# A two-layer attention backbone: which engine makes the high parts of the second output weights

## The chip, the cores and the metric

One core of a Trainium2 chip runs the whole program. The metric is the device time of one execution in microseconds (us). TensorE (PE) multiplies, VectorE (DVE), ScalarE (ACT) and GpSimd (POOL) work on tiles of 128 partitions in SBUF, SyncE (SP) issues transfers. Each engine runs its own instructions strictly in the order in which they are written; engines wait for each other through semaphores that count up.

## The reference, cut to what matters

```python
for l in range(DEPTH):                                  # two layers
    h = x * (1.0 + sc) + sh                             # 1024 latent tokens, hc: 256 context tokens
    q, k, v, z = jnp.split(h @ w_in[l], 4, axis=-1)
    ...
    # layer 1: 8 heads, two softmax maps each, 1280 keys
    s = jnp.einsum('bhmqd,bhmkd->bhmqk', q, k).astype(jnp.float32) * scale
    p = jax.nn.softmax(s, axis=-1)
    a = (p[:, :, 0] - lam * p[:, :, 1]).astype(v.dtype)
    y = jnp.einsum('bhqk,bhkv->bhqv', a, v)             # then an RMS norm per head
    ...
    out = (y * jax.nn.silu(z)) @ w_out[l]               # 1024 x 1024 weights
    x_new = _layer_norm(DEEPNORM_ALPHA * x + (1.0 + g) * out, ln_g[l], ln_b[l])
```

The products with `w_in` and `w_out` are made from split operands: each fp32 matrix is written as a high part of reduced precision (`_hi`) and the rest (`_lo = raw - hi`), and three products (hi·hi, hi·lo, lo·hi) are summed in PSUM.

## The kernel before, in words

The second layer (`differential`) runs in eight chunks, one head each. A chunk projects its q, k, v and gate and then walks over eight query tiles of 128 rows. The last chunk (`last`) has no next chunk to project for, so it prepares the output projection instead: eight row blocks `k` of `w_out` are loaded by SP into two staging slots (`OutWeights.load`, `w_raw`), split into `h_hi[:, k]` and `h_lo[:, k]`, and TensorE begins to multiply with them before the attention is over.

A slot is loaded again only when the block that lay in it has been split: block `k` waits for `ready >= k - 1`, that is for the subtraction of block `k - 2`.

The four engines share the loop over query tiles. I call the stretch of TensorE that begins with the first transposes of query tile `t` "tile t", and the time at which it begins T(t). In it TensorE does, in this order: `turn(3t)` (four transposes of the probabilities of tile t into PSUM bank 6), `scores(0, t+2)`, the rest of the values of tile t-1, `turn(3t+1)` (four), `scores(1, t+2)`, values, `turn(3t+2)` (two), values. In the last two tiles `ahead` takes the place of the scores; in tile 6 it is `after.part(pe, 0, 0, 0, 7)`, 21 products with the weight blocks 0 to 6, each block waited for by `out_w.ready`.

ScalarE copies each group of transposes out of the one bank (`evac`, L1828), since the next group may come only then, and makes the exponentials of both maps (`exp`, L1821). `evac(n)` belongs to `turn(n)`. Its order in tile t is `evac(3t)`, `exp(1, t+1)`, `evac(3t+1)`, `exp(0, t+2)`, `evac(3t+2)`; in the source the loop index is one lower for the first two of them.

VectorE finds row maxima (`row_max`, L1917, from PSUM) and subtracts the maps (`combine`, L1929, which reads two operands from SBUF). Its order in tile t is `row_max(0, t+2)`, `combine(t+1)`, `row_max(1, t+2)`. `turn(3t)` waits for `combine(t)`.

GpSimd, beside that, splits the first four token tiles of the already stored heads (`load_y`, `split_head`) and the eight weight blocks:

```python
for k in range(KT):
    out_w.copy_hi(pool, p, k)      # h_hi = cast(w_raw)
    out_w.split_lo(pool, k)        # h_lo = w_raw - h_hi
    if k == 0:
        after.split_head(pool, 1)
    if k >= KT - 2:
        pool.wait_ge(out_w.ready, k + 1)
        after.load_y(pool, k - (KT - 2) + 2)
```

After the loop come the RMS norm of the second half (`variance(1)`, `normalise(1)`), four transposes (`spread`, L2115) and the output projection (`Project.pe_part`).

Of the kernel before, what the change touches and what calls it, by code (L numbers as in the profile page):

```python
# [20 lines left out]
D = 1024  # L21
# [4 lines left out]
NCH = D // P  # L26
# [34 lines left out]
ACT = mybir.ActivationFunctionType  # L61
# [10 lines left out]
CREDIT = 1  # L72
# [955 lines left out]
class OutWeights:  # L1028
# [10 lines left out]
    def load(self, sp, p, k):  # L1039
# [3 lines left out]
            sp.wait_ge(self.ready, k - 1)  # L1043
        sp.dma_start(self.stage[k % 2], self.w_out[self.l, k * P:(k + 1) * P, :]).then_inc(self.loaded[k % 2], 16)

    def copy_hi(self, pool, p, k):
        if k == 0:
            pool.wait_ge(p.proj, CREDIT + NCH * p.G)
        pool.wait_ge(self.loaded[k % 2], 16 * (k // 2 + 1))
        self.nc.gpsimd.tensor_copy(self.m.h_hi[:, k, 0:D], self.stage[k % 2]).then_inc(self.hi, 1)  # L1050
# [633 lines left out]
def differential(nc, m, far, stack, p, tokens, before, all_counters, out_w, after, rope_in, y_out):  # L1684
# [14 lines left out]
    y_ready, y_stored = sem("y_ready"), sem("y_stored")  # L1699

    NQ = LAT_TILES
    KEYS = TOK_TILES
    turns = [(t, a, min(4, KEYS - a)) for t in range(NQ) for a in range(0, KEYS, 4)]
    TPT = 3
# [5 lines left out]
    sum_of = lambda mp, t: m.stats[:, 32 + t:33 + t] if mp == 0 else stat(t, 3)  # L1710
    first_sums = m.stats[:, 32:32 + NQ]
    COEFS = 2 * NQ + 2
    variances, roots, inv_rms = (m.stats[:, 40 + i * NQ:40 + (i + 1) * NQ] for i in range(3))

    def run():
        with nc.Block() as block:
# [38 lines left out]
            @block.gpsimd  # L1755
            def _(pool):
                before.pool_part(pool)
                p.split_lo_part(pool, nc.gpsimd, 0, 0)
                for g in range(3):
                    for k in range(KT):  # L1760
                        if g == 0:
                            pool.wait_ge(before.mm_done, TOK_TILES + k)
                        tokens.take_hi(pool, g, k)
                pool.wait_ge(rope_loaded, 16)
                with pool.Fori(0, NCH) as c:
                    p.pool_part(pool, c)
                pool.wait_ge(y_stored, CREDIT + 16 * (NCH - 1))
                pool.wait_ge(p.q_ready, CREDIT + NCH * 4)
                after.load_y(pool, 0)
                pool.wait_ge(p.proj, CREDIT + (NCH - 1) * p.G + p.cum[2])  # L1770
                after.split_head(pool, 0)
                pool.wait_ge(after.y_ready, after.ready(0))
                after.load_y(pool, 1)
                for k in range(KT):
                    out_w.copy_hi(pool, p, k)
                    out_w.split_lo(pool, k)
                    if k == 0:
                        after.split_head(pool, 1)
# [3 lines that stand above are left out]
                pool.wait_ge(s_done, CREDIT + NCH * 2 * NQ)  # L1782
                for i in range(2, 4):
                    after.split_head(pool, i)
                pool.wait_ge(y_ready, CREDIT + (NCH - 1) * 2 + 1)
                for i in range(4):
                    after.split_own(pool, i)

            @block.scalar
            def _(act):  # L1790
                for i in range(TOK_TILES - 2):
                    before.act_tile(act, i)
                act.wait_ge(before.mm_done, TOK_TILES - 1)
                p.split_hi_part(act, 0, 0)
                act.wait_ge(before.cols_done, 4)
                for k in range(KT):
                    tokens.modulate(act, 0, k)
                    if k == 1:
                        before.root(act, TOK_TILES - 2)
                    if k == 5:  # L1800
                        before.store(act, TOK_TILES - 2)
                for k in range(KT):
                    tokens.modulate(act, 1, k)
                    if k == 5:
                        act.wait_ge(before.mm_done, before.done(TOK_TILES - 1))
                        p.split_hi_part(act, 0, 1)
                before.root(act, TOK_TILES - 1)
                act.wait_ge(before.stored[1], 16 * 4)
                before.store(act, TOK_TILES - 1)
                p.evacuate(act, 0, 0)  # L1810
                for k in range(KT):
                    tokens.modulate(act, 2, k)
                p.evacuate(act, 0, 1)
                act.wait_ge(p.proj, CREDIT + 4)
                p.evacuate(act, 0, 2)
                before.act_end(act)

                def chunk(c, last):
                    def exp(mp, t):
                        act.wait_ge(max_done, CREDIT + c * 2 * NQ + (2 * t + mp + 1))  # L1820
                        nc.scalar.activation(prob(mp, t), m.banks(3 * mp, 0, TOK), ACT.Exp,  # L1821
                                             bias=stat(t, mp), accum_out=sum_of(mp, t)).then_inc(exp_done, 1)

                    def evac(n):
                        w = turns[n][2] * P
                        act.wait_ge(turned, CREDIT + c * NT + (n + 1))
                        act.wait_ge(av_done, CREDIT + c * NT + max(n - 3, 0))
                        nc.scalar.activation(far.pt[:, n % 4, 0:w], m.bank(6, w), ACT.Copy).then_inc(pt_ready, 1)  # L1828

                    def take_y(half):  # L1830

                        cols = slice(half * 512, half * 512 + 512)
                        act.wait_ge(av_done, CREDIT + c * NT + 4 * TPT * (half + 1))
                        nc.scalar.activation(y_sb[:, cols], m.bank(7), ACT.Copy).then_inc(y_taken, 1)

                    def square(half):

                        cols = slice(half * 512, half * 512 + 512)
                        act.wait_ge(y_taken, CREDIT + c * 4 + 2 * half + 1)
                        nc.scalar.activation(sq[:, cols], y_sb[:, cols], ACT.Square).then_inc(y_taken, 1)  # L1840

                    def root(half):
                        cols = slice(4 * half, 4 * half + 4)
                        act.wait_ge(summed, CREDIT + c * 6 + 3 * half + 2)
                        nc.scalar.activation(roots[:, cols], variances[:, cols], ACT.Sqrt, scale=1.0 / P).then_inc(root_done, 1)

                    p.act_part(act, c, lambda e: e.wait_ge(y_ready, CREDIT + c * 2), lambda e: e.wait_ge(y_stored, CREDIT + c * 16),
                               last)
                    p.late_q_hi(act, c)
                    exp(0, 0)  # L1850
                    exp(1, 0)
                    exp(0, 1)
                    p.gate_tanh(act, c, p.G - 1)
                    evac(0)
                    exp(1, 1)
                    for t in range(NQ):
                        if t == 4:
                            take_y(0)
                        evac(TPT * t + 1)
                        if t + 2 < NQ:  # L1860
                            exp(0, t + 2)
                        evac(TPT * t + 2)
                        if t + 1 < NQ:
                            evac(TPT * t + 3)
                        if t + 2 < NQ:
                            exp(1, t + 2)
                        if t == 5:
                            square(0)
                            root(0)
                        if t == NQ - 2 and not last:  # L1870
                            p.split_hi_part(act, c, 5)
                    take_y(1)
                    square(1)
                    if not last:
                        for j in range(3):
                            p.evacuate(act, c + 1, j)
                    root(1)

                each_chunk(act, chunk)

            @block.vector
# [127 lines left out]
            def _(pe):  # L2009
# [27 lines left out]
                def chunk(c, last):  # L2037
# [23 lines left out]
                    def values(n):  # L2061
# [7 lines left out]
                        for i in range(cnt):  # L2069
                            mm = nc.tensor.matmul(m.psum[:, 7, (t % 4) * P:(t % 4 + 1) * P], far.pt[:, n % 4, i * P:(i + 1) * P],  # L2070
                                                  far.v[:, a + i, :], start=(a + i == 0), stop=(a + i == KEYS - 1))
                        mm.then_inc(av_done, 1)
# [57 lines left out]
class Project:  # L2130
# [30 lines left out]
    def stat(self, i, a, b):  # L2161
        return self.m.stats[:, (i % 2) * 24 + a:(i % 2) * 24 + b]
# [387 lines left out]
```

## Time and profile before

| what | value |
|---|---|
| median of 3 runs | 1750.61 us (1749.9 to 1750.65) |
| the profiled execution | 1750.22 us |
| its span, first to last instruction | 1748.1 us |
| PE busy | 1719.7 us, 98% of the span |
| DVE busy | 1298.0 us, 74% |
| ACT busy | 899.1 us, 51% |
| POOL busy | 374.8 us, 21% |
| last chunk's query tiles 2 to 7 | 1619.78 to about 1661 us of the span |
| output projection alone | 1675.03 to 1740.88 us of the span |

All times below are on the clock of the profiled execution, from its first instruction. The time of an execution is 2.12 us more than its span, for what lies around the instructions. An engine's share of busy time is a mean over stages; which engine ends last in one stage is read from that stage's rows.

### The profile page before, as it was taken

The page shows a single profiled execution, that of the slowest core. Times are in us where ns is not written, and L with a number is a line of the kernel's source. Part 1 is how long each engine was busy: PE and PEld are TensorE (multiplying, and loading weights), DVE is VectorE, ACT ScalarE, POOL GpSimd, SP SyncE. Part 2 cuts the span into 40 slices and gives each one's busy share as a digit, 9 for nine tenths or more (in the row PEclk, how much of TensorE's full clock was granted, in tenths as well). Part 3 has the DMA queues.
Part 4 walks back from the last instruction along what each step waited for, and adds up shares of the span by engine and source line. Part 5 has one row for each costly group of instructions (what it writes and reads, how often), then busy time and mean ns, then how long its engine had stood idle before and what let it go on. Part 6 is the DMA issues. An engine that isn't in the chain of part 4 may idle for free. (4 is left out here: it accounts for less than half of the span.)

```text
span 1748.1 us, 30706 instructions
## 1 busy us (share of the span) xinstructions
PE 1719.7 (98%) x10117; PEld 1495.1 (86%) x10117; DVE 1298.0 (74%) x2289; ACT 899.1 (51%) x1577; POOL 374.8 (21%) x421
## 2 busy tenths in 40 slices
PE   7999999999999999999999999999999999999998
PEld 3898989898989898878878888898988888888887
DVE  6788787878787878739878485857758585857758
ACT  4665656565555555520246465564747374655500
POOL 2221212120202020659220010101010010103951
PEclk9999999999999999999999999999999999999999
DMA  9635252434343433536330110202020201102353
GB/s 360 144 69 135 58 129 62 119 73 115 77 110 79 112 78 87 133 100 203 121 99 13 42 40 19 62 8 73 1 68 12 59 22 38 44 18 73 96 166 120
DMA packets 192216, 150.26 MB, mean 86 GB/s; under 512 B 151042, under 2 KB 159394, under 8 KB 192036
## 3 DMA queue, kind: packets, MB, share of 16 engines
q1 hardware_dynamic: 172964, 119.61, 24.5%
q0 software_dynamic: 16464, 20.52, 5.9%
q10 hardware_dynamic: 2736, 9.44, 1.4%
q8 instruction: 31, 0.51, 0.1%
q14 instruction: 21, 0.17, 0.0%
HBM read 110.73 MB, written 17.79 MB: 74 GB/s over the span
## 5 line engine op out<-in xcount | busy, mean ns | idle before, releaser
L683 PE MATMUL acc<-h_hi,w_hi 128*128 128x512 f32 (+1 forms) x1408 | 522.9, 371 | 4.4 <-DVE h_lo L601 3.0
L683 PE MATMUL acc<-h_hi,w_lo 128*128 128x512 f32 (+1 forms) x1408 | 509.1, 362 | 0.0
L683 PE MATMUL acc<-h_lo,w_hi 128*128 128x512 f32 (+1 forms) x1408 | 508.8, 361 | 0.0
L683 PEld LDWEIGHTS acc<-h_hi,w_hi 128*128 128x128 f32 x1408 | 266.3, 189 | 43.8 <-DVE h_lo L601 4.8
L683 PEld LDWEIGHTS acc<-h_hi,w_lo 128*128 128x128 f32 x1408 | 265.8, 189 | 41.7
L683 PEld LDWEIGHTS acc<-h_lo,w_hi 128*128 128x128 f32 x1408 | 266.7, 189 | 34.6
L1917 DVE TENSOR_REDUCE stats<-acc 128x1 f32<-128x1280 f32 x128 | 189.7, 1487 | 43.3 <-PE acc L2048 41.8
L1821 ACT ACTIVATE far_prob<-acc,stats 128x1280 f32<-128x1280 f32 x128 | 170.3, 1330 | 23.8 <-DVE stats L1917 21.9
L2048 PE MATMUL acc<-k_dup,q_stack 128*128 128x512 f32 (+1 forms) x768 | 176.6, 367 | 1.1 <-ACT far_prob L1821 0.5
L973 POOL TENSOR_TENSOR far_prob<-far_prob,far_rope 128x512 f32<-128x512 f32 x32 | 41.5, 1295 | 631.7 <-DVE far_prob L962 631.7
L1385 ACT ACTIVATE near_pt_hi<-acc 128x384 fp32r<-128x384 f32 (+1 forms) x208 | 110.6, 532 | 125.7 <-PE acc L1591 108.7
L1828 ACT ACTIVATE far_pt<-acc 128x512 f32<-128x512 f32 (+1 forms) x192 | 101.4, 528 | 142.0 <-PE acc L2057 138.9
L2070 PE MATMUL acc<-far_v,far_pt 128*128 128x128 f32 x1280 | 173.4, 275 | 0.0
L2048 PEld LDWEIGHTS acc<-k_dup,q_stack 128*128 128x128 f32 x768 | 135.8, 188 | 33.0 <-ACT far_prob L1821 9.1
L1498 DVE TENSOR_TENSOR near_pt_lo<-acc,near_pt_hi 128x384 fp32r<-128x384 f32 (+1 forms) x208 | 125.9, 605 | 47.2 <-ACT near_pt_hi L1385 45.2
L2070 PEld LDWEIGHTS acc<-far_v,far_pt 128*128 128x128 f32 x1280 | 159.0, 191 | 2.1
L1379 ACT ACTIVATE near_prob<-acc,stats 128x640 f32<-128x640 f32 (+1 forms) x160 | 116.7, 729 | 44.1 <-DVE stats L1473 31.8
L1617 PE MATMUL acc<-near_pt_hi,near_values 128*128 128x256 f32 x416 | 114.2, 303 | 3.0 <-DVE y L1506 2.8
L1591 PE MATMUL acc<-ident,near_prob 128*128 128x128 f32 x704 | 109.4, 273 | 0.1
L1242 POOL DMA_DIRECT2D factor_rows<-near_inverse_turned x112 | 56.3, 510 | 243.6 <-DVE near_inverse_turned L1484 243.6
L1929 DVE SCALAR_TENSOR_TENSOR far_prob<-far_prob,stats 128x1280 f32<-128x1280 f32 x64 | 104.4, 1631 | 2.4 <-DVE stats L1925 0.2
L1617 PE MATMUL acc<-near_pt_lo,near_values 128*128 128x256 f32 x416 | 105.1, 282 | 0.0
(231 smaller groups left out, 2872.9 us busy)
## 6 DMA issues: line engine op xcount, KB each, us to landing
w_raw<-in_w_in SPq DMA_DIRECT2D x64, 512.0 KB, 3.5
near_late_slots<-in_w_mod SPq DMA_DIRECT2D x64, 256.0 KB, 2.8
w_raw<-in_w_out SPq DMA_DIRECT2D x16, 512.0 KB, 3.3
w_raw<-y_t POOLq DMA_DIRECT2D x14, 448.0 KB, 5.5
near_values<-near_values POOLq DMA_DIRECT2D x16, 384.0 KB, 6.3
token_cols<-in_x_cols SPq DMA_DIRECT2D x8, 640.0 KB, 8.2
near_prob<-near_prob SPq DMA_DIRECT2D x128, 40.0 KB, 2.6
far_v<-far_v_blocks SPq DMA_DIRECT2D x128, 40.0 KB, 2.0
```

The source lines that it names most:

```text
L683: mm = nc.tensor.matmul(m.bank(self.bank_of(j, c), w), wt[:, b % 2, k, :], ht[:, k, t0:t0 + w], start=(k == 0 and i == 0), stop=(k == KT - ...
L1379: nc.scalar.activation(probs(i), all_scores(i), ACT.Exp, bias=stat(i, 2), accum_out=stat(i, 3))\
L1385: nc.scalar.activation(turned_part(near.pt_hi, n), turned_bank(n, last), ACT.Copy).then_inc(pt_hi, 1)
L1498: nc.vector.tensor_tensor(turned_part(near.pt_lo, n), turned_bank(n, last), f(turned_part(near.pt_hi, n)), ALU.subtract).then_inc(pt_ready, 1)
L1591: mm = nc.tensor.transpose(turned_bank(n, last)[:, t * P:(t + 1) * P], probs(2 * s + row)[:, a * P:(a + 1) * P], m.ident[:, :])
L1617: mm = nc.tensor.matmul(m.psum[:, 6, u.head * 2 * P:(u.head + 1) * 2 * P], near.values[:, block, u.head, :], pt[:, slot, t * 2 * P:(t + 1) ...
L1821: nc.scalar.activation(prob(mp, t), m.banks(3 * mp, 0, TOK), ACT.Exp, bias=stat(t, mp), accum_out=sum_of(mp, t)).then_inc(exp_done, 1)
L1828: nc.scalar.activation(far.pt[:, n % 4, 0:w], m.bank(6, w), ACT.Copy).then_inc(pt_ready, 1)
L1917: nc.vector.reduce_max(stat(t, mp), m.banks(3 * mp, 0, TOK), AX, negate=True).then_inc(max_done, 1)
L1929: nc.vector.scalar_tensor_tensor(e0, e1, stat(t, 5), e0, ALU.mult, ALU.add).then_inc(p_ready, 1)
L2048: mm = nc.tensor.matmul(m.bank(3 * mp + g, w), m.q_stack[:, mp, t * P:(t + 1) * P], m.k_dup[:, mp, part, k0:k0 + w], start=(part == 0), st ...
L2070: mm = nc.tensor.matmul(m.psum[:, 7, (t % 4) * P:(t % 4 + 1) * P], far.pt[:, n % 4, i * P:(i + 1) * P], far.v[:, a + i, :], start=(a + i = ...
```

## The change

In the last chunk of layer 1 the high parts are no longer made by GpSimd (`copy_hi`) but by ScalarE (`split_hi`), as an `activation` with the function Copy on the same 128x1024 block. ScalarE makes blocks 0 and 1 in the first query tile of its loop and one block in each of the six after it, in each case behind the exponential of the second map. GpSimd waits for the semaphore `hi` and subtracts as before.

```diff
+    def split_hi(self, act, p, k):
+        if k == 0:
+            act.wait_ge(p.proj, CREDIT + NCH * p.G)
+        act.wait_ge(self.loaded[k % 2], 16 * (k // 2 + 1))
+        self.nc.scalar.activation(self.m.h_hi[:, k, 0:D], self.stage[k % 2], ACT.Copy).then_inc(self.hi, 1)
...
+    OUT_SPLITS = {0: (0, 1), 1: (2,), 2: (3,), 3: (4,), 4: (5,), 5: (6,), 6: (7,)}
...
                 for k in range(KT):
-                    out_w.copy_hi(pool, p, k)
                     out_w.split_lo(pool, k)
...
                         if t + 2 < NQ:
                             exp(1, t + 2)
+                        if last:
+                            for k in OUT_SPLITS.get(t, ()):
+                                out_w.split_hi(act, p, k)
                         if t == 5:
                             square(0)
                             root(0)
```

ScalarE before, in tiles 0 and 1 of the last chunk (`far_pt` is an evacuation, `far_prob` an exponential):

```order
L1828 ACTIVATE far_pt<-acc 128x256
L1828 ACTIVATE far_pt<-acc 128x512
L1821 ACTIVATE far_prob,stats<-acc,stats 128x1280
L1828 ACTIVATE far_pt<-acc 128x512
L1821 ACTIVATE far_prob,stats<-acc,stats 128x1280
L1828 ACTIVATE far_pt<-acc 128x256
```

The same place now, and one tile further:

```order
L1834 ACTIVATE far_pt<-acc 128x256
L1834 ACTIVATE far_pt<-acc 128x512
L1827 ACTIVATE far_prob,stats<-acc,stats 128x1280
L1050 ACTIVATE h_hi<-w_raw 128x1024 x2
L1834 ACTIVATE far_pt<-acc 128x512
L1827 ACTIVATE far_prob,stats<-acc,stats 128x1280
L1834 ACTIVATE far_pt<-acc 128x256
L1834 ACTIVATE far_pt<-acc 128x512
L1827 ACTIVATE far_prob,stats<-acc,stats 128x1280
L1050 ACTIVATE h_hi<-w_raw 128x1024
L1834 ACTIVATE far_pt<-acc 128x512
```

The copies of the weights (`h_hi`) stand between the second map's exponential and the next evacuation.

GpSimd before, from the first weight block (`h_hi`, `h_lo`) on; `w_hi`, `w_lo` are the second token tile:

```order
L1050 CAST h_hi<-w_raw 128x1024
L1054 TENSOR_TENSOR h_lo<-w_raw,h_hi 128x1024
L2185 CAST w_hi<-k_raw 128x896
L2187 TENSOR_TENSOR w_lo<-k_raw,w_hi 128x896
L1050 CAST h_hi<-w_raw 128x1024
L1054 TENSOR_TENSOR h_lo<-w_raw,h_hi 128x1024
```

And now, to the end of the weight blocks:

```order
L1060 TENSOR_TENSOR h_lo<-w_raw,h_hi 128x1024
L2194 CAST w_hi<-k_raw 128x896
L2196 TENSOR_TENSOR w_lo<-k_raw,w_hi 128x896
L1060 TENSOR_TENSOR h_lo<-w_raw,h_hi 128x1024 x6
L2186 DMA w_raw<-y_t 128x7x128
L1060 TENSOR_TENSOR h_lo<-w_raw,h_hi 128x1024
L2186 DMA w_raw<-y_t 128x7x128
```

The eight casts are gone from GpSimd; each subtraction now waits for ScalarE. Nothing moves on TensorE, VectorE or SyncE.

## Rows read from the trace of the kernel before

**Rows 1.** Chain that ended last: start us, us, what.
```profile
1675.03 54.65 PE acc L2396 x240
```

**Rows 2.** TensorE timeline, tile 2 and tile 3's begin: start us, us, what, idle before.
```profile
1619.78 0.60 PE L2057 MATMUL acc<-ident,far_prob 128*128 128x128 f32 x4
...
1624.53 0.38 PE L2057 MATMUL acc<-ident,far_prob 128*128 128x128 f32 x2
...
1626.09 0.66 PE L2057 MATMUL acc<-ident,far_prob 128*128 128x128 f32 x4 [0.29 <-DVE far_prob L1929]
```

**Rows 3.** TensorE timeline, first transposes of tiles 4 to 7, block 6, `spread`.
```profile
1632.21 0.60 PE L2057 MATMUL acc<-ident,far_prob 128*128 128x128 f32 x4
...
1638.82 0.66 PE L2057 MATMUL acc<-ident,far_prob 128*128 128x128 f32 x4 [0.58 <-DVE far_prob L1929]
...
1644.94 0.60 PE L2057 MATMUL acc<-ident,far_prob 128*128 128x128 f32 x4
...
1649.50 0.39 PE L2204 MATMUL acc<-h_hi,w_hi 128*128 128x512 f32 x1
...
1653.14 0.60 PE L2057 MATMUL acc<-ident,far_prob 128*128 128x128 f32 x4
...
1666.60 0.60 PE L2115 MATMUL acc<-ident,far_y_sb 128*128 128x128 f32 x4
```

**Rows 4.** ScalarE timeline, the same evacuation in two tiles of the chunk before.
```profile
1541.44 0.60 ACT L1828 ACTIVATE far_pt<-acc 128x512 f32<-128x512 f32 x1 [0.94 <-PE acc L2057]
...
1547.31 0.60 ACT L1828 ACTIVATE far_pt<-acc 128x512 f32<-128x512 f32 x1 [0.94 <-PE acc L2057]
```

**Rows 5.** VectorE and GpSimd timelines, combinations (L1929) and a subtraction of a block.
```profile
1606.54 1.55 DVE L1929 SCALAR_TENSOR_TENSOR far_prob<-far_prob,stats 128x1280 f32<-128x1280 f32 x1
...
1617.41 1.86 DVE L1929 SCALAR_TENSOR_TENSOR far_prob<-far_prob,stats 128x1280 f32<-128x1280 f32 x1
...
1622.30 2.39 POOL L1054 TENSOR_TENSOR h_lo<-w_raw,h_hi 128x1024 fp32r<-128x1024 f32 x1
...
1623.49 2.55 DVE L1929 SCALAR_TENSOR_TENSOR far_prob<-far_prob,stats 128x1280 f32<-128x1280 f32 x1
```

**Rows 6.** Tile w_raw's groups (ns min/median/max), and a copy on ScalarE.
```profile
L1050 POOL CAST h_hi<-w_raw x8: 1035/1047/2306, 1613.4 to 1647.9; 128x1024 fp32r<-128x1024 f32 x8
L1054 POOL TENSOR_TENSOR h_lo<-w_raw,h_hi x8: 2368/2380/3509, 1614.6 to 1649.1; 128x1024 fp32r<-128x1024 f32 x8
...
1556.62 1.05 ACT L655 ACTIVATE w_hi<-w_raw 128x1024 fp32r<-128x1024 f32 x1
```

**Rows 7.** ScalarE timeline, second map's exponentials of tiles 2, 3 and 7.
```profile
1615.04 1.33 ACT L1821 ACTIVATE far_prob<-acc,stats 128x1280 f32<-128x1280 f32 x1
1616.26 0.19 ACT L1821 ACTIVATION_READ_ACCUMULATOR far_prob<-acc,stats 128x1 f32 x1
...
1620.91 1.32 ACT L1821 ACTIVATE far_prob<-acc,stats 128x1280 f32<-128x1280 f32 x1
...
1646.08 1.33 ACT L1821 ACTIVATE far_prob<-acc,stats 128x1280 f32<-128x1280 f32 x1
```

**Rows 8.** Transfers by line: KB each, median us from issue to landing.
```profile
w_raw<-in_w_out SPq DMA_DIRECT2D x6, 512.0 KB, 3.2
```

**Rows 9.** GpSimd and VectorE timelines, near-simultaneous starts in the first layer's output projection.
```profile
808.27 1.97 POOL L2185 CAST k_dup<-w_raw 128x896 fp32r<-128x896 f32 x1
...
816.12 0.94 POOL L2185 CAST w_hi<-w_raw 128x896 fp32r<-128x896 f32 x1
...
808.23 1.22 DVE L2341 SCALAR_TENSOR_TENSOR token_rows<-out_rows,token_rows 128x1024 f32<-128x1024 f32 x1
...
816.15 2.00 DVE L2341 SCALAR_TENSOR_TENSOR token_rows<-out_rows,token_rows 128x1024 f32<-128x1024 f32 x1
```

**Rows 10.** VectorE and GpSimd timelines, normalise(1) and a head's subtraction.
```profile
1664.67 0.69 DVE L1956 TENSOR_TENSOR far_y_sb<-far_y_sb,stats 128x512 f32<-128x512 f32 x1
...
1657.28 2.10 POOL L2187 TENSOR_TENSOR k_dup<-w_raw,k_dup 128x896 fp32r<-128x896 f32 x1
```

## The prediction

> **What bounds the kernel now.** I read the chain that ended last first: from 1675 us on it is TensorE alone [rows 1], so whatever TensorE loses before that time the end loses too. Then I read TensorE's timeline through the last chunk's query tiles, and beside it the other three. The tiles begin at T(2) = 1619.78, T(3) = 1626.09, T(4) = 1632.21, T(5) = 1638.82, T(6) = 1644.94 and T(7) = 1653.14 [rows 2, 3]; tiles 2 to 5 take 6.31, 6.12, 6.61 and 6.12 us. In the chunk before, where GpSimd has nothing to split, the same evacuation comes back after 5.87 us [rows 4]. So the last chunk loses 0.44 + 0.25 + 0.74 + 0.25 = 1.7 us in these four tiles, and the rows say to whom: T(3) and T(5) waited for the combination L1929 on VectorE [rows 2, 3].
>
> Why the combination is late is seen beside GpSimd. Alone it takes 1.55 us. The one at 1623.49 takes 2.55: GpSimd's subtraction, begun at 1622.30, ends at 1624.69, and the combination 1.35 us after that [rows 5]. The two don't share, one waits until the other has ended. Who comes first gets it, down to hundredths: VectorE's start at 808.23 beat GpSimd's at 808.27 (1.97 us for 0.94), and GpSimd's at 816.12 beat VectorE's at 816.15 (2.00 for 1.22) [rows 9]. A GpSimd operation that had to wait ends its own time less 0.15 behind VectorE's end (808.23 + 1.22 = 809.45, then 0.79 to 810.24 for a cast of 0.94), so a subtraction of 2.38 ends 2.23 behind it.
>
> **The change, part by part.** *Casts removed from GpSimd.* Eight casts of 1.05 us (2.3 where blocked) go [rows 6]. None was itself waited for by TensorE; what they can give back is their part of the 1.7 us. That they get cheaper by the move is not so: ScalarE's copy of the same 128x1024 block takes 1.05, GpSimd's cast 1.05 [rows 6]. The Trainium skill (Perfetto Trace Analysis, Optimizing GPSIMD Operations) says to prefer other engines, since GpSimd is generally slower; for this cast the trace shows no difference. By that rule alone the move would be a gain, the relief weighed below.
>
> *Copies added to ScalarE.* In a clean tile the second map's exponential starts at T + 1.13 (1620.91) [rows 2, 7]. It takes 1.22 us to its accumulator read and 0.19 for that, and each instruction starts about 0.1 before the record of the last ends (1615.04 + 1.33 against 1616.26) [rows 7]. So the copy starts 1.31 behind the exponential's start, at T + 2.44, and ends at T + 3.49; the next instruction starts 0.95 behind the copy's start. One copy per tile is free if its data are there: the evacuation of `turn(3t+1)` moves to T + 3.39, the exponential behind it to T + 3.89, and the evacuation of `turn(3t+2)` to T + 5.20, when those transposes, begun at T + 4.75 (1624.53) [rows 2], have just ended.
>
> Two copies in tile 1 are not free. They run 1616.36 to 1617.41 and 1617.31 to 1618.36; `evac(4)` starts at 1618.26, `exp(0,3)` at 1618.76, `evac(5)` 1.31 later at 1620.07 and ends at 1620.46. `turn(6)` needs that bank: T(2) = 1620.50, **+0.7**.
>
> *A wait added to ScalarE: the load of block 2.* This is what the diff doesn't say. A slot is loaded when the subtraction of the block in it is done. Subtraction 0 may start at 1617.46, 0.05 behind its copy; `combine(2)` starts at 1617.41 [rows 5] and is first by 0.05, until 1618.96, so the subtraction ends at 1621.19. The transfer lands 3.2 us later [rows 8]: 1624.45 with the wake-up. ScalarE, in order, stands at copy 2 from 1620.50 + 2.44 = 1622.94 to 1624.45, and behind it stand `evac(7)` (to 1625.40, ending at 1626.00), `exp(0,4)` (1625.90) and `evac(8)` (1627.20, ending at 1627.60). TensorE's `turn(8)` wants the bank at 1625.25 and gets it at 1626.05; T(3) is 1627.65 instead of 1626.37.
>
> *The combination against the subtraction.* In the same tile GpSimd casts and subtracts token tile 1 (0.94 + 2.10) behind subtraction 0, so subtraction 1 starts at 1624.20; `combine(3)` starts at T + 3.71 (1623.49 [rows 5] less 1619.78), now 1624.21. A dead heat; I take GpSimd. Then subtraction 1 ends at 1626.58, the combination at 1627.93, and T(3) = 1627.98: only 0.33 above the other outcome, since both waits run side by side. Shift **+1.9**.
>
> Behind a late combination the second row maximum is late too, the exponential comes at T + 1.38 rather than T + 1.13, and the tile takes 6.12, as tile 3 did before: T(4) = 1634.10. Block 3 lands at 1629.83, before its copy is due at 1630.67. Subtraction 3 is ready at T + 3.79, `combine(4)` at T + 3.71: VectorE first, no cost. Tile 4 starts clean, and GpSimd is ready at T + 3.54, 0.17 before the combination. It wins: ends at T + 5.92, the combination at T + 7.27, T(5) = T(4) + 7.32 = 1641.42. Tile 5 is then a late one, 6.12 again: T(6) = 1647.54, shift **+2.6**. The ends of what one such meeting can cost are 0 (VectorE first) and 7.32 - 5.87 = 1.45 us.
>
> *Block 6 wanted before it is there.* In tile 6 TensorE multiplies with blocks 0 to 6 at once, and comes to block 6 at T + 4.56 (1649.50) [rows 3]. Its copy now ends at T(6) + 1.14 + 1.31 + 1.05 = T + 3.50 (1646.08 for the exponential [rows 7]); the subtraction runs T + 3.55 to T + 5.93, and TensorE goes on at T + 5.98. Nothing covers this: **+1.4**, shift +4.0. Had GpSimd's subtraction been ready by T + 4.56, the term would be nil; for that the copy would have to come 1.4 us earlier.
>
> *Block 7, the heads behind it, and the last half's norm.* Block 7 is copied behind `evac(21)`, which leaves ScalarE free at T(7) + 1.13 as in every tile; its subtraction ends about T(7) + 1.13 + 1.05 + 0.05 + 2.38 = T(7) + 4.6. T(7) is 1653.14 [rows 3] + 4.0, so that is 1661.8. Before, the last block's subtraction started at 1649.1 and took 2.38 [rows 6], and that of token tile 3 came at 1657.28 [rows 10], 5.8 us behind its end; now it comes at about 1667.6, for 2.1 us. `normalise(1)`, at 1664.67 [rows 10], moves to 1668.7 and meets it: it ends at 1670.3 or, should the token tile land 1.4 us later and win the variance's small sum too, at 1671.7. The transposes that need it, 1666.60 [rows 3], are due at 1670.6. Cost 0 to 1.1; I take **+0.6**.
>
> Sum: 0.7 + 1.2 + 0.7 + 1.4 + 0.6 = 4.6 us (the 0.7 in the middle is tile 4, 7.32 against the 6.61 of before). On the profiled execution that is 1750.22 + 4.6; the median of the runs shown lies 0.39 above this execution, so the median to expect is 1750.61 + 4.6 = **1755.2 us**. By itself 0.2% is 3.5 us, about what a measurement of this kernel can tell from no change: faster means under 1747.1, slower over 1754.1.
>
> **The rivals.** *VectorE wins the meetings.* Then T(3) = 1627.65, but subtraction 1 ends later (1627.99), block 3 lands at 1631.24, and ScalarE waits again from 1630.09: T(4) = 1634.44. Tiles 4 and 5 take 5.87: T(6) = 1646.18, +1.2; with block 6 +2.7, with no loss in the tail: 1753.3 us. For it speaks that the leads are small (0.17 us in tile 4); against it that in the rows 0.03 was enough.
>
> *GpSimd wins them all.* `combine(2)` ends at 1621.19 and T(2) is 1621.24, T(3) about 1627.9; then three tiles of 7.32 + 0.25 us put T(6) at 1650.6, +5.7; block 6 comes 0.25 later still, +1.7; with the tail +8.0: 1758.6 us. It takes VectorE's lead of 0.08 in the late tiles turning round.
>
> *Relief: not slower.* The eight casts no longer hold VectorE up, the copies hide in ScalarE's gaps, and the subtractions come between the combinations. Then tiles 2 to 5 fall to 5.87 each, -1.7 us: 1748.9 us. It decides itself at one point, whether block 6 is ready by T(6) + 4.56; by my sum it is 1.4 us late. This is the most the change can give in these tiles, less than 0.2%.
>
> **How the numbers follow.** Forecast 55% (its own range 1753.9 to 1756.2, by the tail's ends and one dead heat), VectorE first 23%, GpSimd first 14%, relief 8%. The time is the forecast's. The range reaches from between relief and VectorE-first to the time of GpSimd-first, 1752.0 to 1758.6, and leaves out relief and half of the last case. Slower by over 0.2%: the forecast but for its lowest part, 0.48, and GpSimd first, 0.14: 0.62. Within 0.2%: 0.35. Faster by over 0.2%: 0.03, for what I have not seen.
>
> **What would show it.** Right: on ScalarE a gap of about 1.5 us before copy 2, ended by the transfer of `w_out`; on TensorE an idle stretch of about 1.4 us in the middle of L2204's first 21 products; combinations of 1.55 and of over 3 us alternating. Wrong: block 2's copy without a wait (then the load rule is not the limit), products with block 6 without a gap, or TensorE later losing its idle time somewhere behind 1675 us, so that the shift does not reach the end. The prediction as a whole falls if the combinations all take 1.55 to 1.9 us and T(6) comes before 1645.

## The result and the profile after

The change makes the kernel slower: 1754.78 us median (1754.07 to 1756.31, 12 runs) against 1750.50 (1749.58 to 1751.01, 12 runs), a ratio of 1.0024 with an interval of 1.0017 to 1.0032. That is 4.3 us, where 4.6 were forecast. The profiled execution after has a span of 1752.1 us.

The chain that ended last is the same piece of TensorE work, only later (start us, us, what), to be read against [rows 1]:

```profile
1678.98 54.65 PE acc L2405 x240
```

So everything was lost before the output projection. In this execution tile 1 begins at 1613.22, 0.43 us earlier than in the one before (1613.65), by what ran ahead of the tiles; lengths of tiles, not times of day, are compared below. TensorE's timeline after, the first transposes of tiles 1 to 7, where it stood still, block 6 and `spread` (the last column is the idle time before, and who ended it):

```profile
1613.22 0.66 PE L2066 MATMUL acc<-ident,far_prob 128*128 128x128 f32 x4
...
1620.13 0.63 PE L2066 MATMUL acc<-ident,far_prob 128*128 128x128 f32 x4 [0.28 <-ACT far_pt L1834]
...
1625.70 0.41 PE L2066 MATMUL acc<-ident,far_prob 128*128 128x128 f32 x2 [0.63 <-ACT far_pt L1834]
...
1627.54 0.66 PE L2066 MATMUL acc<-ident,far_prob 128*128 128x128 f32 x4 [0.53 <-DVE far_prob L1938]
...
1633.65 0.60 PE L2066 MATMUL acc<-ident,far_prob 128*128 128x128 f32 x4
...
1640.99 0.65 PE L2066 MATMUL acc<-ident,far_prob 128*128 128x128 f32 x4 [0.97 <-DVE far_prob L1938]
...
1647.11 0.60 PE L2066 MATMUL acc<-ident,far_prob 128*128 128x128 f32 x4
...
1653.10 0.50 PE L2213 MATMUL acc<-h_hi,w_hi 128*128 128x512 f32 x1 [1.28 <-POOL h_lo L1060]
...
1656.87 0.60 PE L2066 MATMUL acc<-ident,far_prob 128*128 128x128 f32 x4
...
1670.50 0.66 PE L2124 MATMUL acc<-ident,far_y_sb 128*128 128x128 f32 x4
```

Against [rows 2, 3], and tile 1 begun at 1613.65 before:

| stretch | before, us | after, us | difference | what is seen there after |
|---|---|---|---|---|
| tile 1 | 6.13 | 6.91 | +0.78 | two copies ahead of one evacuation |
| tile 2 | 6.31 | 7.41 | +1.10 | load of block 2, combination late |
| tile 3 | 6.12 | 6.11 | -0.01 | |
| tile 4 | 6.61 | 7.34 | +0.73 | combination behind subtraction 4 |
| tile 5 | 6.12 | 6.12 | 0 | |
| tile 6 | 8.20 | 9.76 | +1.56 | block 6 not ready |
| tile 7 to `spread` | 13.46 | 13.63 | +0.17 | `normalise(1)` behind GpSimd |
| sum | 52.95 | 57.28 | +4.33 | |

ScalarE's timeline after, its exponential ahead of copy 2, the copy and what stood behind it:

```profile
1621.29 1.32 ACT L1827 ACTIVATE far_prob<-acc,stats 128x1280 f32<-128x1280 f32 x1
1622.51 0.20 ACT L1827 ACTIVATION_READ_ACCUMULATOR far_prob<-acc,stats 128x1 f32 x1
1624.02 1.06 ACT L1050 ACTIVATE h_hi<-w_raw 128x1024 fp32r<-128x1024 f32 x1 [1.31 <-DMA w_raw<-in_w_out]
1624.98 0.58 ACT L1834 ACTIVATE far_pt<-acc 128x512 f32<-128x512 f32 x1
```

ScalarE waited 1.31 us for the transfer; the evacuation behind it, which TensorE needed, had nothing to do with weights. VectorE's combinations after (start us, us):

```profile
1623.86 3.62 DVE L1938 SCALAR_TENSOR_TENSOR far_prob<-far_prob,stats 128x1280 f32<-128x1280 f32 x1
...
1631.30 1.55 DVE L1938 SCALAR_TENSOR_TENSOR far_prob<-far_prob,stats 128x1280 f32<-128x1280 f32 x1
...
1637.37 3.56 DVE L1938 SCALAR_TENSOR_TENSOR far_prob<-far_prob,stats 128x1280 f32<-128x1280 f32 x1
...
1644.75 1.55 DVE L1938 SCALAR_TENSOR_TENSOR far_prob<-far_prob,stats 128x1280 f32<-128x1280 f32 x1
```

and GpSimd's subtractions (x2 stands for those of blocks 1 and 2, of which the first begins at 1623.76, 0.10 ahead of the combination; the second by itself is in the second view):

```profile
1623.76 5.96 POOL L1060 TENSOR_TENSOR h_lo<-w_raw,h_hi 128x1024 fp32r<-128x1024 f32 x2
1631.36 3.73 POOL L1060 TENSOR_TENSOR h_lo<-w_raw,h_hi 128x1024 fp32r<-128x1024 f32 x1 [1.64 <-ACT h_hi L1050]
1637.22 2.36 POOL L1060 TENSOR_TENSOR h_lo<-w_raw,h_hi 128x1024 fp32r<-128x1024 f32 x1 [2.13 <-ACT h_hi L1050]
1644.81 3.72 POOL L1060 TENSOR_TENSOR h_lo<-w_raw,h_hi 128x1024 fp32r<-128x1024 f32 x1 [5.23 <-ACT h_hi L1050]
```
```profile
1626.08 3.64 POOL L1060 TENSOR_TENSOR h_lo<-w_raw,h_hi 128x1024 fp32r<-128x1024 f32 x1
```

In each of the tiles 2 to 5 a combination and a subtraction start within 0.15 us of each other, and the earlier one always runs its own time (1.55 us on VectorE, about 2.4 on GpSimd) while the other is stretched to over 3.5. The earlier one is GpSimd by 0.10 and 0.15 in tiles 2 and 4, VectorE by 0.06 in tiles 3 and 5.

### The profile page after: what moved, and what is told of

It is laid out like the page before. It is cut to its first block and busy times, and to the rows that moved or that the text cites. A ratio compares the mean times of both kernels' runs of the same rounds, so it can differ in the third digit from the quotient of the medians.

```text
span 1752.1 us, 30706 instructions
## 1 busy us (share of the span) xinstructions
PE 1720.4 (98%) x10117; PEld 1495.7 (85%) x10117; DVE 1297.6 (74%) x2289; ACT 905.9 (52%) x1585; POOL 365.9 (21%) x413
```

## The experiments

Three readings were set against each other. A: the loss is made of waits at named places, those of the table. B: ScalarE has become too full, and each of its eight copies costs its share wherever it stands. C: only the meetings of VectorE and GpSimd matter. All times are medians against the kernel before in the same session; the ratio is estimated from all runs and can differ a little from the quotient of two medians. Of the edits that hand a cast back to GpSimd, the bookkeeping of semaphores is left out.

**Blocks 0 and 1 back on GpSimd.**

```diff
...
-    OUT_SPLITS = {0: (0, 1), 1: (2,), 2: (3,), 3: (4,), 4: (5,), 5: (6,), 6: (7,)}
+    OUT_SPLITS = {1: (2,), 2: (3,), 3: (4,), 4: (5,), 5: (6,), 6: (7,)}
...
                 for k in range(KT):
+                    if k in (0, 1):
+                        out_w.copy_hi(pool, p, k)
                     out_w.split_lo(pool, k)
```

> Blocks 0 and 1 are cast by GpSimd again, ScalarE makes only blocks 2 to 7, where it made them. Theory A (named waits: two copies in one tile, the load of block 2, the meeting of subtraction and combination, block 6 on TensorE): the first two terms go, since subtraction 0 ends near 1617 again and block 2 lands near 1620, before its copy; one meeting of about 1.4 us late in the loop and the 1.4 to 1.5 us before block 6 stay. About +2.8 us over the kernel before. Theory B (ScalarE is simply too full, each copy costs about an eighth of the loss): six of eight copies left, +3.2 us, with the loss spread over all tiles. Theory C (only the meetings with VectorE matter): +4.3 us, as in the changed kernel.

Measured: 1753.55 against 1750.54 us, +3.0, ratio 1.0018 (1.0009 to 1.0027). The time alone doesn't tell A from B here, the tiles do. They begin at 1613.55, 1619.67, 1626.01, 1632.13, 1639.47, 1645.62 and 1655.37, so tiles 1 to 6 take 6.12, 6.34, 6.12, 7.34, 6.15 and 9.75: the first three are those of before to 0.03 us, and tiles 4 and 6 are those of the changed kernel. Copy 2 stands on ScalarE without a wait:

```profile
1622.10 1.06 ACT L1051 ACTIVATE h_hi<-w_raw 128x1024 fp32r<-128x1024 f32 x1
```

Tiles 2, 3 and 5 hold a copy and are no longer than before, which is against B; the loss in tile 6 is TensorE's wait for the subtraction of block 6 and has no combination in it, which is against C.

```profile
1651.61 0.50 PE L2219 MATMUL acc<-h_hi,w_hi 128*128 128x512 f32 x1 [1.29 <-POOL h_lo L1064]
```

**Block 6 later on TensorE.**

```diff
-                            after.part(pe, 0, j, 0, KT - 1)
+                            after.part(pe, 0, j, 0, KT - 2 if j == 0 else KT - 1)
+                            if j == 1:
+                                after.part(pe, 0, 0, KT - 2, KT - 1)
```

> The changed kernel, but TensorE takes only blocks 0 to 5 in tile 6 and block 6 behind the products of tile 7. Theory A: no gap in front of block 6; tile 6 is then ended by the seventh combination, which the variance's small sum holds up, so some 0.3 us of the 1.5 come back as another wait: 1.1 to 1.3 us less than the changed kernel, about +3.1 us over before. Theories B and C: nothing to gain, +4.3 us.

Measured: 1753.68 us, +3.1, ratio 1.0018 (1.0009 to 1.0027); 1.1 us less than the changed kernel, with the same meetings as there, which is against C. The gap before block 6 is gone, tile 6 takes 7.99 us instead of 9.76 (0.68 of that are the three products moved to tile 7), and a smaller wait has come up in it, though not the one expected: the last transposes of tile 6 wait for ScalarE, whose square root behind copy 6 waits for the variance, with an evacuation behind it (ScalarE's timeline, then TensorE's).

```profile
1654.17 0.21 ACT L1851 ACTIVATE stats<-stats 128x4 f32<-128x4 f32 x1 [0.69 <-DVE stats L1951]
1654.28 0.58 ACT L1834 ACTIVATE far_pt<-acc 128x512 f32<-128x512 f32 x1
```
```profile
1655.01 0.41 PE L2066 MATMUL acc<-ident,far_prob 128*128 128x128 f32 x2 [0.34 <-ACT far_pt L1834]
```

**Small subtractions.** GpSimd subtracts 128 of 1024 columns per block of the second layer; the low parts of the other columns are left out.

```diff
-        self.nc.gpsimd.tensor_tensor(self.m.h_lo[:, k, 0:D], self.stage[k % 2], f(self.m.h_hi[:, k, 0:D]),
+        n = P if self.l else D
+        self.nc.gpsimd.tensor_tensor(self.m.h_lo[:, k, 0:n], self.stage[k % 2][:, 0:n], f(self.m.h_hi[:, k, 0:n]),
```

> The changed kernel, but GpSimd subtracts only the first 128 of the 1024 columns of each block of the second layer; the low parts of the other columns are left out. ScalarE's eight copies and TensorE's products are all there. Theory A: no load wait, no long meeting, block 6 in time; of the terms only the two copies in one tile stay, 0.4 to 0.7 us, and the tiles otherwise take 5.87: 0.8 us under the kernel before. Theory B: the copies are the cost, so still +3 us or more. Theory C: -1 us or so as well; e2 tells it from A.

Measured: 1750.03 against 1750.54 us, -0.5, ratio 0.9997 (0.9988 to 1.0006). With all eight copies on ScalarE the kernel is no slower than before, so B falls. Tiles 1 to 5 take 6.91, 5.87, 5.86, 6.20 and 5.89: tile 1 keeps its excess, the two copies, and tile 4 keeps 0.33 us over a clean tile; there ScalarE has the evacuation of half of y to do beside the copy, and the last transposes start that much later in the tile. In the other tiles a copy costs nothing.

```profile
1613.87 0.66 PE L2067 MATMUL acc<-ident,far_prob 128*128 128x128 f32 x4
...
1620.78 0.63 PE L2067 MATMUL acc<-ident,far_prob 128*128 128x128 f32 x4 [0.28 <-ACT far_pt L1835]
```

**Copy 4 half a microsecond later.**

```diff
-    OUT_SPLITS = {0: (0, 1), 1: (2,), 2: (3,), 3: (4,), 4: (5,), 5: (6,), 6: (7,)}
+    OUT_SPLITS = {0: (0, 1), 1: (2,), 2: (3,), 4: (5,), 5: (6,), 6: (7,)}
...
                         if t == 4:
                             take_y(0)
+                            if last:
+                                out_w.split_hi(act, p, 4)
```

> The changed kernel, but block 4's copy stands behind the evacuation of the first half of y instead of ahead of it, so its subtraction comes 0.5 us later and VectorE's combination comes first in tile 4. Theory A with meetings that alternate: tile 4 falls from 7.3 to about 6.0 us, but tile 5 now starts clean, GpSimd is 0.17 us ahead there and tile 5 rises from 6.1 to 7.3; block 6 comes 0.25 us later. Sum: 0 to +0.3 us against the changed kernel, about +4.5 over before. If meetings don't hang together: -1.3 us, about +3.0 over before. Theory B: +4.3.

Measured: 1755.55 us, +5.0, ratio 1.0029 (1.0018 to 1.0039). Tile 4 falls to 6.19, tile 5 rises to 7.37, and tile 6 takes 10.00 instead of 9.76. The meeting has moved by one tile (combination and subtraction of tile 5):

```profile
1644.05 3.58 DVE L1940 SCALAR_TENSOR_TENSOR far_prob<-far_prob,stats 128x1280 f32<-128x1280 f32 x1
```
```profile
1643.92 2.37 POOL L1060 TENSOR_TENSOR h_lo<-w_raw,h_hi 128x1024 fp32r<-128x1024 f32 x1 [2.30 <-ACT h_hi L1050]
```

So the meetings hang together, as A says: a tile in which VectorE lost is followed by one in which it wins, because its late row maximum holds ScalarE's exponential and with it the next copy back.

**Block 1 alone back on GpSimd.**

```diff
...
-    OUT_SPLITS = {0: (0, 1), 1: (2,), 2: (3,), 3: (4,), 4: (5,), 5: (6,), 6: (7,)}
+    OUT_SPLITS = {0: (0,), 1: (2,), 2: (3,), 3: (4,), 4: (5,), 5: (6,), 6: (7,)}
...
+                    if k in (1,):
+                        out_w.copy_hi(pool, p, k)
                     out_w.split_lo(pool, k)
```

> The changed kernel, but block 1 is cast by GpSimd, so that ScalarE makes one copy instead of two in the first tile. Theory A: tile 1 loses 0.7 us less, but copy 2 then only waits 0.7 us longer for its load, and GpSimd's extra cast makes the loads behind it later: nothing gained, 0.5 to 1 us more than the changed kernel, about +5.0 over before, with a second load wait before copy 3. Theory B, and any reading in which the two copies' 0.7 us add to the load's wait: 0.5 to 0.7 us less than the changed kernel, about +3.7.

Measured: 1758.22 against 1750.36 us, +7.9, ratio 1.0044 (1.0031 to 1.0058; 5 runs). The direction is A's and the size is not: tile 1 is back at 6.13, and tiles 2 and 3 take 8.19 and 7.78, with load waits of 2.37 and 1.94 us on ScalarE.

```profile
1624.74 1.06 ACT L1051 ACTIVATE h_hi<-w_raw 128x1024 fp32r<-128x1024 f32 x1 [2.37 <-DMA w_raw<-in_w_out]
...
1632.53 1.06 ACT L1051 ACTIVATE h_hi<-w_raw 128x1024 fp32r<-128x1024 f32 x1 [1.94 <-DMA w_raw<-in_w_out]
```

One copy less on ScalarE costs 3.4 us by the medians. The profiled execution, at 1756.53 us, is one of the two fastest of the five, which reach to 1759.61; its span is 2.4 us longer than that of the changed kernel's, and from tile 1 to `spread` it takes 59.17 us against 57.28, 1.9 more. What the slower executions lose besides, no trace shows. Tiles 1 and 2 together take 14.32 us in both kernels: what tile 1 gives back, the longer wait for block 2 takes. Most of the loss is in tile 3 (7.78 us for 6.11), and there the load chain is the reason: GpSimd's cast of block 1 was blocked by the combination and took 2.30 us for 1.05, which puts subtraction 1 and with it the load of block 3 back.

```profile
1624.26 2.30 POOL L1057 CAST h_hi<-w_raw 128x1024 fp32r<-128x1024 f32 x1
```

**All copies in the gap.** The same eight copies, each moved behind the evacuation of two transposes, that is one evacuation and one exponential earlier.

```diff
-    OUT_SPLITS = {0: (0, 1), 1: (2,), 2: (3,), 3: (4,), 4: (5,), 5: (6,), 6: (7,)}
+    OUT_SPLITS = {}
+    EARLY_SPLITS = {0: (0, 1), 1: (2,), 2: (3,), 3: (4,), 4: (5,), 5: (6,), 6: (7,)}
...
                         evac(TPT * t + 2)
+                        if last:
+                            for k in EARLY_SPLITS.get(t, ()):
+                                out_w.split_hi(act, p, k)
                         if t + 1 < NQ:
                             evac(TPT * t + 3)
```

> The changed kernel with all eight copies moved from behind the second map's exponential into the gap behind the evacuation of two transposes, blocks 0 and 1 in the first tile, then one per tile. Theory A: the copies are free there, the late meetings vanish and block 6 is ready in time; what stays is the wait for the load of block 3 (about 1 us) and a meeting in tile 2: +0.1 us over before (0 to +0.8). Theory B: eight copies as in the changed kernel, +4.3 us. If the place behind the exponential doesn't matter, also +4.3.

Measured: 1750.54 against 1750.36 us, +0.2, ratio 1.0001 (0.9992 to 1.0010). On balance the loss is gone, with nothing changed but the place of the copies. Tiles 3 to 6 take 6.12, 5.87, 5.87 and 8.19, so tiles 4 and 5 are clean and block 6 is ready in time. What stays is in tiles 1 and 2 (6.72 and 6.81, 0.59 and 0.50 over the kernel before); what tiles 4 and 5 give back (0.74 and 0.25) pays for it. In tile 1 two copies again stand together. In tile 2 a combination starts while GpSimd is subtracting blocks 1 and 2, and TensorE waits for it:

```profile
1624.26 3.06 DVE L1942 SCALAR_TENSOR_TENSOR far_prob<-far_prob,stats 128x1280 f32<-128x1280 f32 x1
```
```profile
1627.37 0.66 PE L2070 MATMUL acc<-ident,far_prob 128*128 128x128 f32 x4 [0.79 <-DVE far_prob L1942]
```

Copy 3 waits for its load as expected, but at the seam of tiles 2 and 3, and tile 3 is no longer for it than any tile behind a late combination (6.12):

```profile
1627.05 1.06 ACT L1050 ACTIVATE h_hi<-w_raw 128x1024 fp32r<-128x1024 f32 x1 [0.94 <-DMA w_raw<-in_w_out]
```

**Mixed, three or four copies on ScalarE in that gap.** GpSimd casts blocks 0, 2, 3, 5 and 7 in the first kernel, shown here; in the second it casts 0, 3, 5 and 7, and ScalarE also copies block 2, under index 2 of `EARLY_SPLITS`.

```diff
...
-    OUT_SPLITS = {0: (0, 1), 1: (2,), 2: (3,), 3: (4,), 4: (5,), 5: (6,), 6: (7,)}
+    OUT_SPLITS = {}
+    EARLY_SPLITS = {0: (1,), 4: (4,), 5: (6,)}
...
                 for k in range(KT):
+                    if k in (0, 2, 3, 5, 7):
+                        out_w.copy_hi(pool, p, k)
                     out_w.split_lo(pool, k)
...
                         evac(TPT * t + 2)
+                        if last:
+                            for k in EARLY_SPLITS.get(t, ()):
+                                out_w.split_hi(act, p, k)
```

> GpSimd casts blocks 0, 2, 3, 5 and 7 itself; ScalarE copies only 1, 4 and 6, behind the evacuation of two transposes, where it waits about 0.9 us for TensorE's next transposes anyway: block 1 in the first tile of its loop, 4 in the fifth, 6 in the sixth. Theory A: no load is waited for, subtractions fall beside row maxima and not on combinations (block 4's and 6's end before the next one), block 6 is ready in time; tiles 3 to 5 take 5.87 and the 1.7 us that the kernel before loses come back: -1.9 us against before, about 1748.6. Theory B (each copy on ScalarE costs some 0.5 us): +1.6 us.

> As e5_mix, but block 2 too is copied by ScalarE, in the same gap of the third tile of its loop. Theory A: also -1.9 us against before, a copy in the gap being free. Theory B: +2.2 us, half a us more than e5_mix.

Measured, with three copies: 1749.46 against 1750.36 us, -0.9, ratio 0.9997 (0.9988 to 1.0006). With four: 1748.61, -1.8, ratio 0.9993 (0.9984 to 1.0002). Both profiles have a span of 1746.6 us, 1.5 under before, and from tile 1 to `spread` they take 51.26 and 51.24 us for the 52.95 of before: the 1.7 us are back. Tiles 4, 5 and 6 begin, with four copies, at

```profile
1631.70 0.60 PE L2076 MATMUL acc<-ident,far_prob 128*128 128x128 f32 x4
...
1637.57 0.60 PE L2076 MATMUL acc<-ident,far_prob 128*128 128x128 f32 x4
...
1643.43 0.60 PE L2076 MATMUL acc<-ident,far_prob 128*128 128x128 f32 x4
```

that is 5.87 and 5.86 us apart, the length of a tile with no disturbance [rows 4]. The fourth copy cost nothing that these runs show. The four-copy kernel was measured once more:

> The kernel of e5b_mix once more against the kernel before, since its interval of 0.9984 to 1.0002 just holds 1. By the spans of the profiles (1746.6 against 1748.1 us) -1.5 us, a ratio of 0.9991; if the first measurement was a chance, 1.0000.

Measured: 1749.15 against 1750.67 us, -1.5, ratio 0.9991 (0.9982 to 1.0000). Its profile has a span of 1747.8 us, only 0.3 under before, though from tile 1 to `spread` it again takes 1.5 us less (51.46); the rest was lost ahead of the tiles (0.4 us) and behind them. Twice the median is 1.5 to 1.8 us lower and twice the interval reaches 1: probably a small gain over the kernel before, not more than that; over the changed kernel it is some 6 us.

## Why the prediction was right

The prediction is taken here point by point, in its own steps. **Two copies in tile 1**: +0.7 forecast, +0.78 in the trace; the small-subtraction kernel shows it with no other loss than the 0.33 us of tile 4. **The load of block 2**: a wait of 1.5 us was forecast on ScalarE and 1.31 came, `turn(8)` waited as said, and tile 2 grew by 1.10 where the sum had 1.2. The two terms are not separate losses, though: with block 1 back on GpSimd tile 1 is shorter, and tiles 1 and 2 together take the same 14.32 us, since the load then holds ScalarE longer. **The dead heat** of subtraction 1 and `combine(3)` went to GpSimd, as taken, by 0.10 us. That was luck in part: the sum had the two 0.01 us apart, and by its own rival the other outcome gives 1753.3 us. **The meetings** came in tiles 2 and 4 and not in 3 and 5; tile 4 took 7.34 us for a forecast 7.32. That this is one mechanism and not two accidents is shown by the kernel in which copy 4 moves 0.5 us and the loss moves a tile. The Trainium skill (SBUF — State Buffer, Who interferes with whom) says that a VectorE instruction with two SBUF inputs contends with a GpSimd instruction that reads SBUF, that the port pair they share is an exclusive lock, and that the order of issue decides who is blocked; the trace agrees, down to recorded starts 0.06 us apart. **Block 6**: +1.4 forecast; the first product with block 6 begins 5.99 us into tile 6, where 5.98 was forecast and 4.56 was measured before. The gap on TensorE is 1.28 us and the tile grew by 1.56. Moving block 6 gave 1.1 us back, not the whole, for the reason shown there.

The one term that was clearly mis-sized is **the tail**: 0.6 was taken out of 0 to 1.1, and 0.17 came. `normalise(1)` was blocked as forecast (2.05 us for 0.69), but it ended at 1670.44, when TensorE, whose last product ahead of the transposes began at 1670.09, had only just become free:

```profile
1668.39 2.05 DVE L1965 TENSOR_TENSOR far_y_sb<-far_y_sb,stats 128x512 f32<-128x512 f32 x1
```
```profile
1667.74 2.16 POOL L2196 TENSOR_TENSOR k_dup<-w_raw,k_dup 128x896 fp32r<-128x896 f32 x1
```

The other four terms are off by 0.03 to 0.16 us each. Of the rivals, VectorE-first and GpSimd-first each describe tiles that exist, but not the run as a whole. Relief was not wrong about the place of the 1.7 us: the mixed kernels bring it back. It was wrong about these copies, whose place made the subtractions start just ahead of the combinations and block 6 come late.

## What to carry to other kernels

When a step moves to an engine that runs in order, look at what the step itself waits for and at what stands behind it there: here a copy of weights, waiting for a transfer, held up an evacuation that had nothing to do with weights. Where two engines exclude each other, the phase of the step in the loop can decide more than its engine: with the same eight copies on ScalarE the kernel is 4.3 us slower when they stand behind the exponential, and 0.2 us, within the noise, when they stand one evacuation and one exponential earlier. A relieved engine is worth only what was lost to it, so work that out first; here it was 1.7 us, while tiles 2 and 6 alone grew by 2.7.

## What had not been expected

That taking one of two adjacent copies away makes the kernel slower by more than the two had cost (1758.22 us against 1754.78): the forecast for it was 0.5 to 1 us. In the trace 1.7 us of it come from one load that lands later: when the two staging slots come free matters more here than how many instructions ScalarE has.
